# RWKV mixing layer in a fused fp32 block stack: ScalarE's factor and copy steps reordered, and the r times k products moved from VectorE to GpSimd

## What is computed

```python
r = xr @ w_rkv[0]; k = xk @ w_rkv[1]; v = xv @ w_rkv[2]
decay = jnp.exp(-jnp.exp(w.astype(f32)))
a = jax.nn.sigmoid(a0 + (xa @ a1) @ a2)
kk = heads(k * k_k); kk = kk / norm(kk)
k = k * (1.0 + (a - 1.0) * k_a)
def step(S, inp):
    sa = jnp.einsum('bhij,bhj->bhi', S, -kk_t)
    S = (S * w_t[:, :, None, :] + sa[..., None] * b_t[:, :, None, :]
         + v_t[..., None] * k_t[:, :, None, :])
    y = jnp.einsum('bhij,bhj->bhi', S, r_t)
    return S, y
bonus = jnp.sum(r_h * k_h * r_k.astype(f32), axis=-1, keepdims=True) * v_h
```

## Time and profile before

| | us |
|---|---|
| median of 3 runs | 2931.18 |
| lowest to highest | 2929.32 to 2931.43 |
| the profiled execution | 2929.32 |
| its span, first to last instruction | 2927.3 |

### The profile page before, as it was taken

The page is one execution under the profiler, slowest core; times in us unless marked ns, Lnnn a source line. Parts: engine busy times, 40 slices in busy tenths (PEclk is TensorE's granted clock), DMA queues, the critical chain, the costliest instruction groups (busy, mean ns, idle before and its releaser), DMA issues.

```text
span 2927.3 us, 49011 instructions
## 1 busy us (share of the span) xinstructions
PE 2728.5 (93%) x18522; PEld 2202.9 (75%) x18522; DVE 1086.8 (37%) x1624; ACT 610.9 (21%) x1157; POOL 1766.6 (60%) x1823
## 2 busy tenths in 40 slices
PE   8999978988778899999899998889999989999998
PEld 6888866767773678888788887768888877777677
DVE  3332053874443343320533312565243124022245
ACT  2110034324331121100211101252111001244111
POOL 6777767763310467777577775666677755645565
PEclk9999979989996899999899999899999998999998
DMA  4333313210000223333233332323333322322212
GB/s 133 96 97 94 97 36 86 78 47 4 4 4 0 65 73 96 97 94 97 61 97 94 96 97 76 112 105 99 88 96 96 95 79 75 94 62 65 81 40 80
DMA packets 116796, 226.02 MB, mean 77 GB/s; under 512 B 13088, under 2 KB 13856, under 8 KB 115616
## 3 DMA queue, kind: packets, MB, share of 16 engines
q1 hardware_dynamic: 114624, 209.46, 25.4%
q10 hardware_dynamic: 2016, 14.22, 1.3%
HBM read 221.53 MB, written 2.10 MB: 76 GB/s over the span
## 4 chain that ended last, share of the span: by engine, by line
PE 85%; DVE 6%; issue 3%; POOL 3%; ACT 3%; DMA 1%; SPq 0%; DVEq 0%; POOLq 0%; ACTq 0%
PE bank L221 22%; PE bank L223 22%; PE bank L222 22%; PE bank L299 2%; POOL turn_a L1804 1%; PE bank L1128 1%; PE bank L332 1%; DVE acc L295 1%; PE bank L1146 1%; PE bank L1082 1%; PE bank L2056 1%; PE bank L1143 1%; POOL w_raw L1266 1%; PE bank L2047 1%; PE bank L2238 1%
## 5 line engine op out<-in xcount | busy, mean ns | idle before, releaser
L207 POOL TENSOR_TENSOR w_lo<-w_raw,w_hi 128x512 fp32r<-128x512 f32 x778 | 1041.1, 1338 | 903.9 <-PE bank L223 831.3
L221 PE MATMUL bank<-x_hi,w_hi 128*128 128x512 f32 x2064 | 820.6, 398 | 28.9 <-POOL w_lo L207 13.0
L223 PE MATMUL bank<-x_hi,w_lo 128*128 128x512 f32 x2064 | 817.0, 396 | 0.0
L222 PE MATMUL bank<-x_lo,w_hi 128*128 128x512 f32 x2064 | 813.0, 394 | 0.0
L212 POOL TENSOR_SCALAR w_hi<-w_raw 128x512 fp32r<-128x512 f32 x778 | 562.9, 723 | 5.0 <-DMA w_raw<-weights 5.0
L221 PEld LDWEIGHTS bank<-x_hi,w_hi 128*128 128x128 f32 x2064 | 392.6, 190 | 117.5 <-issue 11.4
L222 PEld LDWEIGHTS bank<-x_lo,w_hi 128*128 128x128 f32 x2064 | 392.4, 190 | 87.3
L223 PEld LDWEIGHTS bank<-x_hi,w_lo 128*128 128x128 f32 x2064 | 392.2, 190 | 86.5
L520 DVE TENSOR_TENSOR f<-bank,rstd 128x512 f32<-128x512 f32 x88 | 56.7, 686 | 611.4 <-PE bank L223 605.6
L223 PE MATMUL bank<-mid_hi,w_lo 128*128 128x512 f32 x704 | 276.7, 393 | 0.0
L221 PE MATMUL bank<-mid_hi,w_hi 128*128 128x512 f32 x704 | 275.4, 391 | 0.8 <-POOL w_lo L207 0.8
(11 more groups left out here) (393 smaller groups left out, 3289.9 us busy)
## 6 DMA issues: line engine op xcount, KB each, us to landing
w_raw<-weights SPq DMA_DIRECT2D x778, 256.0 KB, 2.6
ada_w<-ada_in ACTq DMA_DIRECT2D x8, 1536.0 KB, 6.6
h<-xT SPq DMA_DIRECT2D x4, 512.0 KB, 7.3
out<-f SPq DMA_DIRECT2D x8, 256.0 KB, 2.1
mask_b<-mask_b_in ACTq DMA_DIRECT2D x1, 640.0 KB, 5.0
spread<-spread_in SPq DMA_DIRECT2D x1, 512.0 KB, 7.5
window<-window_in ACTq DMA_DIRECT2D x1, 512.0 KB, 3.7
masks<-masks_in SPq DMA_DIRECT2D x1, 320.0 KB, 6.8
```

The lines of the kernel that those rows point to most:

```text
L207: pool.tensor_tensor(w_lo[:, (n - 1) % RW, :], w_raw[:, (n - 1) % RS, :], w_hi[:, (n - 1) % RW, :].bitcast(F32), ALU.subtract).then_inc(w_ ...
L221: pe.matmul(o, w_hi[:, s, c], hi, start=first, stop=False)
L222: pe.matmul(o, w_hi[:, s, c], lo, start=False, stop=False)
L223: done = pe.matmul(o, w_lo[:, s, c], hi, start=False, stop=last)
```

## The change

1. ScalarE runs `r_out(0)` ahead of `factors(2)`, no longer behind it.
2. ScalarE runs `v_out(1)` ahead of `factors(7)`, no longer behind it.
3. The eight products r times k are made by GpSimd in quad 0, two behind the fills of each of the levels 1 to 4, into two buffers instead of four. Product k waits for bonus matmul k - 2 from k = 2 on. VectorE no longer makes them.

```diff
-        rk = [sb(f"rk_{home}", [P, T], at=where[home]) for home in ("acc", "reset", "wa_hi", "diag")]
+        rk = [sb("rk0", [P, T], at=where["acc"]), sb("rk1", [P, T], at=where["reset"])]
...
             factors(0)
             factors(1)
+            r_out(0)
             factors(2)
-            r_out(0)
             for q in range(16, 19):
                 tile(q)
...
             factors(6)
+            v_out(1)
             factors(7)
-            v_out(1)
...
-        RK_AT = (0, 1, 2, 3, 0, 1, 0, 1)
-        RK_AFTER = {("z", 0, l, 1): range(2 * l - 2, min(2 * l, KT)) for l in LEVELS}
...
         cg = Steps("core_pool", [s_ for m in range(QUADS) for s_ in [("blank", m, u, p) for u in two for p in two] +
-                                            [t_ for l in LEVELS for t_ in ["zero"] * ((m, l) == (0, 3)) + [(n, m, l, u) for n in ("e", "fill") for u in two]]])
+                                            [t_ for l in LEVELS for t_ in ["zero"] * ((m, l) == (0, 3)) + [(n, m, l, u) for n in ("e", "fill") for u in two] +
+                                             [("rk", k) for k in (2 * l - 2, 2 * l - 1) if m == 0 and k < KT]]])
...
-                    pe.wait_ge(*cv("rk", m))
-                    pe.matmul(z_bank[0][0:HEADS, :], r_gather[:, m, :], rk[RK_AT[m]][:], start=m == 0, stop=m == KT - 1).then_inc(*cp.tell(*st))
+                    pe.wait_ge(*cg("rk", m))
+                    pe.matmul(z_bank[0][0:HEADS, :], r_gather[:, m, :], rk[m % 2][:], start=m == 0, stop=m == KT - 1).then_inc(*cp.tell(*st))
...
+                    for k in (2 * l - 2, 2 * l - 1):
+                        if m == 0 and k < KT:
+                            if k >= 2:
+                                pool.wait_ge(*cp("bonus", k - 2))
+                            pool.tensor_tensor(rk[k % 2][:], r_arr[:, k, :], k_arr[:, k, :], ALU.mult).then_inc(*cg.tell("rk", k))
...
-                    for k in RK_AFTER.get(st, ()):
-                        if k >= 4:
-                            dve.wait_ge(*cp("bonus", RK_AT[k] + (2 if k >= 6 else 0) * 2))
-                        dve.tensor_tensor(rk[RK_AT[k]][:], r_arr[:, k, :], k_arr[:, k, :], ALU.mult).then_inc(*cv.tell("rk", k))
```

More of the change, by code:

```diff
@@ L658, in program @@
                    [(n, m) for n in ("k", "sq") for m in range(4)] + [(n, m) for n in ("k", "sq") for m in range(4, KT)] + [("sg", m) for m in each] + ["norm"] + [("a", m) for m in each] +
-                   [(n, k) for k in range(3) for n in FACTORS] + [("r", m) for m in range(4)] + [(n, 3) for n in FACTORS] +
+                   [(n, k) for k in (0, 1) for n in FACTORS] + [("r", m) for m in range(4)] + [(n, k) for k in (2, 3) for n in FACTORS] +
                    [("r", m) for m in range(4, KT)] + [(n, k) for k in (4, 5) for n in FACTORS] + [("v", 0, t) for t in range(TT)] +
-                   [(n, k) for k in (6, 7) for n in FACTORS] + [("v", 1, t) for t in range(TT)])
+                   [(n, 6) for n in FACTORS] + [("v", 1, t) for t in range(TT)] + [(n, 7) for n in FACTORS])
         PREP = "cum cm fl kk k2 b K B A0 A".split()
@@ L1017, in program @@
         ca = Steps("core_act", [s_ + (i,) for s_ in STAGES for i in range(1 if s_ == ("bonus", KT - 1) else ON_ACT.get(s_[0], 0))])
-        RK_AT = (0, 1, 2, 3, 0, 1, 0, 1)
-        RK_AFTER = {("z", 0, l, 1): range(2 * l - 2, min(2 * l, KT)) for l in LEVELS}
-        cv = Steps("core_dve", [t_ for s_ in STAGES for t_ in [s_ + (i,) for i in ((1, 0) if s_[0] == "first" else range(ON_DVE.get(s_[0], 0)))] + [("rk", k) for k in RK_AFTER.get(s_, ())]])
+        cv = Steps("core_dve", [s_ + (i,) for s_ in STAGES for i in ((1, 0) if s_[0] == "first" else range(ON_DVE.get(s_[0], 0)))])
         cg = Steps("core_pool", [s_ for m in range(QUADS) for s_ in [("blank", m, u, p) for u in two for p in two] +
-                                            [t_ for l in LEVELS for t_ in ["zero"] * ((m, l) == (0, 3)) + [(n, m, l, u) for n in ("e", "fill") for u in two]]])
+                                            [t_ for l in LEVELS for t_ in ["zero"] * ((m, l) == (0, 3)) + [(n, m, l, u) for n in ("e", "fill") for u in two] +
+                                             [("rk", k) for k in (2 * l - 2, 2 * l - 1) if m == 0 and k < KT]]])
         def half(j):
```

## The result

| kernel | median us | lowest to highest | runs |
|---|---|---|---|
| before | 2931.3 | 2929.32 to 2933.07 | 4 |
| changed | 2951.55 | 2947.56 to 2956.09 | 4 |

The changed kernel takes 1.0069 times as long, 95% interval 1.0052 to 1.0087: 20 us slower, between 15 and 26. The forecast was 2948 in 2942 to 2957. Both intervals hold 1.0070 to 1.0087, which is 20 to 25 us.

A forecast was written before the change was run, and what follows sets the result against it. TensorE is busy 93%, but in the changed stretch the chain runs through VectorE, TensorE, then the inverse's levels. Terms 2.9 + 4.6 + 9.6 = 17.1 us on 2929.3 gave 2946.4, plus 1.9 for the median: 2948, range 2942 to 2957.

The forecast's parts named there:

- if the clock is 0.5 after level 2: Sign set beforehand: the prediction is wrong if TensorE's granted clock is 0.5 after level 2 of quad 0.
- likeliest case: Whole kernel: stall, late gate and e_mat waits add 17.1 us at a holding clock; 2942 to 2956, chance 0.55.
- the rival to which it gave 0.25: Clock falls in the 4.4 us gap before level 3: level 3 at half clock, 3 to 5 us more, 2952; chance 0.25.
- Part 1, 2.9 us: r_out(0) ahead of factors(2): VectorE stalls 5.1 us for the gate of tile 2 and gets 2.2 back.
- 1.2 us a unit: VectorE at tile 2: time recovered per GpSimd weight unit split during the stall; 1.85 units give 2.2 us back.
- Part 2, 4.6 us: v_out(1) ahead of factors(7): the gate of tile 7 waits, so GpSimd's first e_mat starts at 638.05 instead of 633.41.
- the 4.0 us for k2 to the end of the query product: VectorE at tile 7: this stretch takes 4.0 us without GpSimd's splits beside it, instead of 6.9.
- Part 3, waits, 9.6 us: Quad 0: z products of levels 3, 4 and 5 wait for e_mat behind GpSimd's products, 4.4, 2.6 and 2.6 us.
- Faster: Rival: VectorE's products hold up TensorE's second x product; four levels would free 6 us, 2925; chance 0.04.
- nothing: Rival: all costs under 5.9 us, each beside a wait taken for short; about 2933; chance 0.04.
- Part 3 alone: Rival: VectorE recovers the whole tile 2 stall and the tile 7 tail overlaps; only 9.6 us, 2941; chance 0.07.
- parts 1 and 2 alone: Rival: bonus matmul reports early or e_mat still hides, so only the ScalarE moves cost: 7.5 us, 2939; chance 0.05.

The follow-up runs named there:

- the second measurement: The changed kernel measured once more, nothing altered: 2957.98 us against 2928.91 for the kernel before, 1.0090 times (1.0070 to 1.0110).
- the extra matmuls: Kernel before with only the GpSimd products edit, plus unread 64x512 matmuls on TensorE behind bonus matmuls 1, 3 and 5: 1.0022 times before.
- the products behind e_mat: Kernel before with only the GpSimd products edit, each pair queued behind both e_mat of the next level, two buffers: 1.0000 times before.
- part 3 with four buffers: Kernel before with only the GpSimd products edit, but keeping four buffers, so products wait for bonus matmuls only from k = 4: 1.0009 times before.

## Why the prediction was right, and where it was not

The forecast, 2948 in 2942 to 2957, holds the measured 2951.55, and the direction was right. The median of the second measurement, 2957.98, lies 1 us outside. That the first came within 4 us is in good part luck. The sum of 17.1 us left out 10.1 us of clock and had part 1 too dear by 1.5 to 2.6, against 24 to 27 us in the stages of the two profiles, and the first measurement, 20 us, fell low. Parts 2 and 3 were read rightly as waits, but by the prediction's own sign, "if the clock is 0.5 after level 2", its likeliest case is wrong: the rival to which it gave 0.25 is what took place.

- **Part 1, 2.9 us: mis-sized.** The stall was right to a few hundredths (5.08 for 5.1). What comes back is 3.7 to 4.8 us, not 2.2, so 0.3 to 1.4 us are left at `v_out(0)`. The term that failed is the 2.2 us, "1.2 us a unit" for the 1.85 units that pass during the stall. Some 2.3 us do come back up to the scan of tile 3, but another 1.35 in the preparation of tile 3 (all three profiles with part 1), and in the first profile of the changed kernel 1.6 more behind the scan of tile 4. Which of VectorE's instructions are stretched by which split was not settled.
- **Part 2, 4.6 us: right.** 4.53 in three profiles, with the 4.0 us for k2 to the end of the query product there too (640.88 to 644.16 + 0.68 = 3.96).
- **Part 3, waits, 9.6 us: right.** 4.36, 2.62 and 2.62, and 10.2 for all of part 3 that the extra matmuls did not take away. The GpSimd product took 1.26 to 1.28 us for an assumed 1.27. That VectorE's relief is worth nothing is shown by the products behind e_mat.
- **Part 3, the clock: the step that failed.** "I lean to a clock that holds" with 0.25 for the rival, and 3 to 5 us for it, from the first gap only. The clock fell behind all three waits, and it costs 10.1 us. The row against me stood in the text: a wait of 2.91 us ahead of level 1, with half clock behind it. I gave each wait a price as if it were alone, and asked only of the longest whether the clock would fall. The Trainium skill's section that the prediction drew on, TensorE: Matmul & The Clock Gate, Part 1, pointed the right way, and the profiles agree: 0.98 in the wait and 0.58 for the 12 us behind it. The rival's own number, 2952, is near the measured time by chance as well, since it counted one fall at 3 to 5 us, and three came, 10.1 us together.
- **Rivals.** Faster and nothing are refuted by both intervals. "Part 3 alone" and "parts 1 and 2 alone" are refuted by the stages: parts 2 and 3 both cost in full, and part 1 costs about 1 us.

By the profiles the change is 0.3 to 1.4 + 4.5 + 10.2 + 10.1 = 25 to 26 us, and between 1.3 less and 1.2 more by B in the two profiles of the changed kernel, as the clock behind the wait for `v_out(0)` has it.

## What to carry to other kernels

An operation handed to an idle engine is not free if it waits there: what counts is what stands behind it in that engine's queue, and a product that waits for step n must not stand ahead of what step n + 1 needs. Before moving a transfer or a copy ahead of other work on an in-order engine, look whether it is already waiting for its source; if it is, the move gains nothing, and the work behind it pays. In this kernel each new idle gap of TensorE among small matmuls had two prices, its own length and the slower clock behind it, and over the three gaps the second was as large as the first.

## What the runs showed of the hardware

- A single wait of 2.62 us between stages of small matmuls, with the clock at full ahead of it, was enough for the granted clock to go from full to half (part 3 with four buffers: 0.50 for the 6 us behind it, a z product of 1.92 us for 1.12). The Trainium skill, TensorE: Matmul & The Clock Gate, Part 1, tells of such a fall after idle time.
- Extra matmuls whose results nobody reads made part 3 10 us faster: the clock stayed at 1.00 through waits that stood anyway, where it had been at half for 27.3 us.
- Stages that were not touched repeated to 0.03 us between kernels and executions (A and C of the table), while the first stretch of the kernel, up to `r_out(0)`, varied by 10.7 us. Whole executions of the kernel before took 2920 to 2944 us, so that their medians could hardly tell 0.1%, and stage times could.
